# A mixture-of-experts schedule in which one more pair of experts works on gathered rows

## The reference, cut to what matters

```
scores = sigmoid(xt @ router_w)
biased = (scores + router_b).reshape(T, 4, 4)
best_group = argmax(top_k(biased, 2).sum(-1))         # one of four groups
local = top_k(biased of the best group, 2)            # two of its four experts
gate = scores of the two / their sum
y[token] += gate * ((silu(x @ w_gate[e]) * (x @ w_up[e])) @ w_down[e])
```

## Times and profile before

| | us |
|---|---|
| median of three runs | 1383.17 (1382.49 to 1383.35) |
| the profiled execution, its own time | 1383.31 |
| its span, first to last instruction | 1381.4 |
| TensorE busy in the span | 1321.1 (96%) |
| VectorE busy | 926.4 (67%) |
| ScalarE busy | 694.1 (50%) |
| expert pairs of layer 0, from the first matmul of pair 0's second tile to the first down of pair 7 | 194.2 |
| the same stretch of layer 1 | 195.4 |

### The profile page before, as it was taken

The page is one execution under the profiler, slowest core; times in us unless marked ns, Lnnn a source line. Parts: engine busy times, 40 slices in busy tenths (PEclk is TensorE's granted clock), DMA queues, the critical chain, the costliest instruction groups (busy, mean ns, idle before and its releaser), DMA issues.

```text
span 1381.4 us, 18142 instructions
## 1 busy us (share of the span) xinstructions
PE 1321.1 (96%) x7377; PEld 727.5 (53%) x7384; DVE 926.4 (67%) x1138; ACT 694.1 (50%) x710; POOL 99.3 (7%) x56
## 2 busy tenths in 40 slices
PE   6999999989999999999999999999989989999996
PEld 4686555446644445555667555444445545454442
DVE  5686776877764676465567575676866767766666
ACT  5466565335543454344457343555634664455552
POOL 0000000000000031000033003000004000300000
PEclk9999999999999999999999999999999999999999
DMA  9475434646665736475610445777927305576882
GB/s 308 138 249 159 146 122 158 223 160 205 211 207 194 254 134 224 162 252 191 207 62 2 153 153 183 242 252 234 351 100 266 110 0 186 180 229 231 271 270 96
DMA packets 152652, 258.07 MB, mean 187 GB/s; under 512 B 8881, under 2 KB 81532, under 8 KB 152572
## 3 DMA queue, kind: packets, MB, share of 16 engines
q1 hardware_dynamic: 152572, 256.96, 55.4%
HBM read 255.87 MB, written 1.07 MB: 186 GB/s over the span
## 4 chain that ended last, share of the span: by engine, by line
PE 84%; DVE 8%; DMA 2%; ACT 2%; issue 2%; DVEq 1%; POOL 1%; SPq 0%; POOLq 0%; ACTq 0%
PE ps L1192 15%; PE ps L1008 12%; PE ps L726 11%; PE ps L707 8%; PE ps L1273 6%; PE ps L1010 6%; PE ps L1031 6%; DVE w_ring L1883 3%; PE ps L744 3%; PE ps L968 2%; PE ps L1250 2%; PE ps L1128 1%; PE ps L671 1%; PE ps L1303 1%; ACT w_hi L1454 1%
## 5 line engine op out<-in xcount | busy, mean ns | idle before, releaser
L1883 DVE SCALAR_TENSOR_TENSOR w_ring<-w_ring,w_hi 128x2048 f16<-128x2048 f32 (+2 forms) x206 | 460.8, 2251 | 161.3 <-ACT w_hi L1454 160.1
L1454 ACT ACTIVATE w_hi<-w_ring 128x2048 f16<-128x2048 f32 (+2 forms) x206 | 381.5, 1864 | 220.7 <-PE ps L1031 50.9
L1008 PE MATMUL ps<-actT,w_hi 128*128 128x512 f16 x640 | 208.2, 379 | 1.1 <-issue 1.1
L1010 PE MATMUL ps<-actT,w_ring 128*128 128x256 f16 x640 | 174.4, 273 | 0.0
L1454 ACT ACTIVATE arena<-ps 128x512 f16<-128x512 f32 (+8 forms) x95 | 64.5, 694 | 168.0 <-PE ps L1010 76.6
L1192 PE MATMUL ps<-w_ring,arena 128*128 128x512 f16 x384 | 145.5, 379 | 0.0
L726 PE MATMUL ps<-w_hi,actT 128*128 128x512 f16 x448 | 137.1, 382 | 2.9 <-DVE w_ring L1883 2.9
L1192 PE MATMUL ps<-w_hi,arena 128*128 128x512 f16 x448 | 139.1, 379 | 0.0
L707 PE MATMUL ps<-w_hi,actT 128*128 128x512 f16 (+2 forms) x384 | 113.8, 373 | 2.9 <-DVE actT L1888 2.9
L1008 PEld LDWEIGHTS ps<-actT,w_hi 128*128 128x128 f16 x640 | 62.6, 98 | 77.1 <-issue 1.6
L1192 PE MATMUL ps<-arena 128*128 128x512 f16 x320 | 99.1, 379 | 0.0
(11 more groups left out here) (430 smaller groups left out, 1897.1 us busy)
## 6 DMA issues: line engine op xcount, KB each, us to landing
w_ring<-in_dil_w_in SPq DMA_DIRECT2D x36, 1024.0 KB, 5.2
w_ring<-in_w_ff SPq DMA_DIRECT2D x32, 1024.0 KB, 5.1
w_ring<-in_exp_w_gate SPq DMA_DIRECT2D x64, 512.0 KB, 4.2
w_ring<-in_exp_w_up SPq DMA_DIRECT2D x64, 512.0 KB, 5.2
w_ring<-in_exp_w_down SPq DMA_DIRECT2D x32, 1024.0 KB, 5.5
w_ring<-in_w_in SPq DMA_DIRECT2D x24, 1024.0 KB, 5.1
w_ring<-in_sb_w_in SPq DMA_DIRECT2D x12, 1024.0 KB, 5.7
w_ring<-in_w_branch SPq DMA_DIRECT2D x8, 1024.0 KB, 5.0
```

Source lines behind the costliest of these rows:

```text
L1008: pe.matmul(ps[:, bank + c, :], w_h[:, k, cols], aT[:, kk, :], start=(kk == 0), stop=False, skip_group_check=True)
L1010: ins = pe.matmul(ps[:, bank + c, 0:S], w_l[:, k, cols], aT[:, kk, 0:S], start=False, stop=(kk == KD - 1), skip_group_check=True)
L1454: return act.activation(dst, src, ACT.Copy, scale=scale)
L1883: dve.scalar_tensor_tensor(out=lo16(h)[:, 0:kn * c], in0=w_ring[:, h % RING, 0:kn * c], scalar=W_POW, in1=hi16(h)[:, 0:kn * c], op0=ALU.mu ...
```

## The change

The pairs become `0TXYAYZZ`. Pair 0 is still the first half of group 0 on all tokens. T is a half of the group that most tokens chose, and A is one more pair on all tokens: the other half of the top group, or of group 1 where the top group is group 0. X is the second half of group 0 (of group 1 in that case), on gathered rows, and Y and Z are the pairs of the other two groups, on gathered rows. So three pairs are full and five are few, and the gathered rows lie in three blocks of 128 (X, Y, Z) where there were two.

- The top group must be known before pair 1's gate and up weights can be loaded. `counts` moves ahead in pair 0 and waits for `r_best`; `top_group`, seven dependent instructions on VectorE ahead of `weigh(0, 0)`, writes the five group numbers; SP waits for them after the load of the second down of pair 0. The long ranking in `route` goes.
- In pair 0 the splits 6 and 7, which are the halves of pair 1's first `gate_up`, move behind `h_high(1, 0)` and `h_low(1, 0)`.
- `turn_slots` and two copies on ScalarE become `slot_rows` on TensorE and `slot_tokens`, four comparisons of 256 columns, on VectorE.
- Six gathers of 16 records with 128 columns replace four gathers of 8 records with 256 columns. The last two come behind pair 2's first `gate_up_few` and behind pair 1's second `down`. `gathered(5)` stands in pair 2 on both ScalarE and VectorE, ahead of the splits 4 and 5.
- In VectorE's `pair` the splits move as in ScalarE's, which is shown.

```diff
-GROUP_RANK = (0, 0, 2, 1, 2, 1, 3, 3)
-GROUP_PAIR = (0, 1, 0, 0, 1, 1, 0, 1)
-FIRST_FEW = 2
+PAIR_GROUP = "0TXYAYZZ"
+PAIR_HALF = (0, 1, 1, 0, 0, 1, 0, 1)
+SLOT_GROUPS = "XYZ"
+GROUP_NAMES = "TAXYZ"
+GROUP_TABLE = ((0, 4, 8, 12), (4, 4, 8, 12), (4, 0, 0, 0), (8, 8, 4, 4), (12, 12, 12, 8))
+GATHERS = 1
+GATHER_BANKS = (5, 4, 7, 6, 7, 6)
+ROUTE_PE = {"counts": 1, "tokens": 2, "rows": (3, 4, 5, 7, 8, 9), "gates": 6}
+ROUTE_DVE = {"best": 1, "groups": 2, "slots": 3, "tokens": 4, "rows": 5}
 
 
 def few(j):
 
-    return GROUP_RANK[j] >= 2
+    return PAIR_GROUP[j] in SLOT_GROUPS
...
-                    if GROUP_RANK[j] and len(group) == 1:
-                        sp.wait_ge(sig("route_dve"), 6 * layer + ROUTE_DVE["groups"])
-                        for r in range(3):
-                            group.append(sp.value_load(group_at[0:1, r:r + 1], min_val=4, max_val=12))
+                    if j == 2:
+                        for name in "XYAZ":
+                            group_load(name)
                     if few(j):
                         gate_up(j, 0)
                         down(j - 1, 1)
                     else:
                         if j:
                             down(j - 1, 1)
+                        if j == 1:
+                            sp.wait_ge(sig("route_dve"), 10 * layer + ROUTE_DVE["groups"])
+                            group_load("T")
                         gate_up(j, 0)
...
-                    c = GROUP_RANK[j] - 2
+                    c = block_of(j)
+                    if b == 0:
+                        gathered(2 * c + 1)
                     for i in range(2):
-                        if j == FIRST_FEW and b == 0:
-                            pe.wait_ge(sig("route_dve"), 6 * layer + ROUTE_DVE["rows"] + 2 * i + 1)
...
                     if b == 0 and slot_pairs(j):
-                        pe.wait_ge(sig("moe_y_lo"), 3 * layer + slot_pairs(j))
+                        pe.wait_ge(sig("moe_y_lo"), 4 * layer + slot_pairs(j))
+                    elif b == 0:
+                        pe.wait_ge(sig("route_dve"), 10 * layer + ROUTE_DVE["rows"] + 5)
...
                 def counts():
 
+                    pe.wait_ge(sig("route_dve"), 10 * layer + ROUTE_DVE["best"])
...
+                def slot_rows():
+
+                    pe.wait_ge(sig("route_dve"), 10 * layer + ROUTE_DVE["slots"])
+                    for t in range(T):
+                        ins = pe.matmul(ps[:, 5, t * P:(t + 1) * P], r_slot[:, t:t + 1].broadcast_to([P, P]), ident,
+                                        start=True, stop=True)
+                    ins.then_inc(sig("route_pe"), 1)
...
+                def gather(q):
+
+                    c = slice(q // 2 * P, (q // 2 + 1) * P)
+                    for i in range(4):
+                        k = 4 * (q % 2) + i
                         for t in range(T):
+                            ins = pe.matmul(ps[:, GATHER_BANKS[q], i * P:(i + 1) * P], x_tok[:, t, k * P:(k + 1) * P],
+                                            slot_of[:, t, c], start=(t == 0), stop=(t == T - 1))
...
                 def gather_gates():
-                    pe.wait_ge(sig("route_dve"), 6 * layer + ROUTE_DVE["rows"])
-                    for c in range(2):
+                    for c in range(3):
...
                         gate_up(j, 0, 1, True)
+                        counts()
                         gate_up(j, 1, 1, True, (0,))
                         turn(0, j)
-                        counts()
                         gate_up(j, 1, 1, True, (1,))
+                        pe.wait_ge(sig("route_dve"), 10 * layer + ROUTE_DVE["groups"])
+                        empty(3)
                     else:
-                        if j == 1:
-                            pe.wait_ge(sig("route_dve"), 6 * layer + ROUTE_DVE["slots"])
                         gate_up(j, 0, 1, True)
                         if by_slots(j - 1):
                             to_tokens(j - 1)
                         gate_up(j, 1, 0)
                         turn(0, j)
                         if gathers:
-                            turn_slots()
+                            slot_rows()
                         gate_up(j, 1, 1, True)
                     if j == NE // 2 - 1:
                         down(0, j, (0,))
...
                         down(1, j, (1,))
                         return
                     if gathers:
-                        pe.wait_ge(sig("route_act"), 5 * layer + ROUTE_ACT["tokens"])
+                        pe.wait_ge(sig("route_dve"), 10 * layer + ROUTE_DVE["tokens"])
                         pe.wait_ge(sig("x_full"), 2 * layer + 2)
                         gather(0)
                     put = down_few if by_slots(j) else down
...
                     if gathers:
                         gather(1)
                         gather(2)
+                        gathered(0)
+                        gather_gates()
                         pe.wait_ge(sig("moe_hT"), NE * layer + 2 + j * 2)
                         gather(3)
-                        gather_gates()
                     if few(j + 1):
                         gate_up_few(j + 1, 0)
                     else:
                         gate_up(j + 1, 0, 0)
+                    if gathers:
+                        gathered(2)
+                        gather(4)
                     put(1, j)
+                    if gathers:
+                        gathered(3)
+                        gather(5)
...
-                    gathers = j == FIRST_FEW - 1
+                    gathers = j == GATHERS
                     if j and by_slots(j - 1) and not few(j):
                         y_high(j - 1)
                     silu(0, j)
+                    if j == GATHERS + 1:
+                        gathered(5)
                     if j and by_slots(j - 1) and few(j):
                         y_high(j - 1)
                     split(4, j)
                     split(5, j)
                     h_high(0, j)
-                    if gathers:
-                        act.wait_ge(sig("route_pe"), 7 * layer + ROUTE_PE["tokens"])
-                        copy(tok16, ps[:, 5, :].rearrange("p (c s) -> p c s", c=2), SUM_POW / A_POW)
-                        copy(tok_of, ps[:, 5, S:2 * S]).then_inc(sig("route_act"), 1)
-                    next_split(6, j)
-                    if gathers or few(j):
+                    if j:
+                        next_split(6, j)
+                    if j == 0 or gathers or few(j):
                         silu(1, j)
                         if gathers:
                             gathered(0)
-                        next_split(7, j)
+                        if j:
+                            next_split(7, j)
                     else:
                         next_split(7, j)
                         silu(1, j)
                     if few(j):
                         next_split(8, j)
                     h_high(1, j)
+                    if j == 0:
+                        next_split(6, j)
+                        next_split(7, j)
                     if gathers:
                         for q in range(1, 4):
                             gathered(q)
                     if not few(j):
                         next_split(8, j)
+                    if gathers:
+                        gathered(4)
                     next_split(9, j)
...
+                def top_group():
+
+                    dve.wait_ge(sig("route_pe"), 9 * layer + ROUTE_PE["counts"])
+                    dve.tensor_copy(r_cnt, ps[:, 3, 0:12])
+                    dve.drain()
+                    dve.scalar_tensor_tensor(out=r_n, in0=rank0[:, 0, :], scalar=0.125, in1=r_cnt[:, 8:12],
+                                             op0=ALU.mult, op1=ALU.add)
+                    dve.drain()
+                    dve.tensor_reduce(r_max, g4(r_n), AX.X, ALU.max)
+                    dve.drain()
+                    dve.tensor_tensor(r_top, r_n, r_max.broadcast_to([P, 4]), ALU.is_ge)
+                    dve.drain()
+                    dve.tensor_tensor(g4(r_prod), group_table, r_top.unsqueeze(1).broadcast_to([P, 13, 4]), ALU.mult)
+                    dve.drain()
+                    dve.tensor_reduce(r_tab, g4(r_prod), AX.X, ALU.add)
+                    dve.drain()
+                    dve.tensor_copy(group_at[:, :], r_tab[:, 0:5]).then_inc(sig("route_dve"), 1)
...
+                def slot_tokens():
+                    dve.wait_ge(sig("route_pe"), 9 * layer + ROUTE_PE["tokens"])
+                    for c in range(3):
+                        dve.tensor_scalar(tok16[:, c, :], ps[:, 5, 0:S], slot_at[:, c:c + 1], SUM_POW / A_POW,
+                                          ALU.is_equal, ALU.mult)
+                    dve.tensor_scalar(tok_of, ps[:, 5, 0:S], slot_at[:, 2:3], None, ALU.is_equal)\
+                        .then_inc(sig("route_dve"), 1)
...
                     h_low(0, j)
+                    if gathers:
+                        slot_tokens()
...
```

(31 more changed lines are left out.)

129 lines of the change are left out of this document (62 added, 67 removed).

## The result

| | us |
|---|---|
| before, median of seven runs | 1381.91 (1380.39 to 1383.35) |
| after, median of seven runs | 1386.58 (1385.62 to 1388.61) |
| ratio | 1.0036, 95% interval 1.0025 to 1.0048 |
| profiled execution after, its own time and its span | 1388.02, 1386.2 |

The change makes the kernel slower by 0.36% by the ratio; the medians are 4.7 us apart. The forecast was 1382.8, no measurable change. So the time was missed by 3.8 us and the change by 5.2: -0.5 was forecast, +4.7 came. The profiled span grew by 4.8 us (1381.4 to 1386.2).

A forecast was written before the change was run, and what follows sets the result against it. TensorE's queue was taken to bound the expert stretches. Work -20.7, waits +15.6, landings +1.2 and clock +3.4 sum to -0.5 us, from 1383.31 to 1382.8 us; the range for 8 in 10 was 1379.3 to 1386.8.

The forecast's parts named there:

- The work: TensorE in both expert layers: fewer matmuls and shorter turns, less larger gathers and gates, -10.4 us per layer, -20.7 in all.
- top_group: Pair 0: seven VectorE instructions delay weigh(0, 0) to about 812.2; TensorE waits 1.8 us, with 0.15 at the turn before.
- the prediction's 0.17: Amount by which a wait's real delay exceeds its profile bracket, from one wait of 0.97 us that really was 1.13.
- The moved splits: Pair 0: splits 6 and 7 behind h_high and h_low delay pair 1's first gate_up by 4.9 us per layer.
- GpSimd's x_tok starts earlier and is not late: Pair 0: claim that GpSimd's x_tok starts earlier and is not late; no time was put down for it.
- The clock: Behind pair 0's 5 us wait the clock halves for 3.4 us, losing 1.7 us per layer, 3.4 in all.
- shorter waits lose the clock too: Rival, chance 0.13: waits of 2.1 us (pair 2) and 1.8 (pair 0) lose 1.7 each; two of four give 1386.2 us.
- Few behind few: Few pair after a few pair by slots, 2-3, 5-6 and 6-7: delays of 0.9, 1.0 and 0.3 us per layer.
- Landings: Few pairs: weight halves land late by a few tenths and push ScalarE; 1.2 us taken, bounds 0 and 3.
- the 7.0 of before: Old kernel's TensorE delays over both layers, 2.33 + 3.29 + 1.4 us, subtracted from the new waits of 22.6.
- The rival that the clock holds: Rival, chance 0.22: clock stays full through both layers' long waits, 1378.2 us, or 1379.4 with late landings.
- The DMA rival: Rival, chance 0.07: the five few pairs starve TensorE at 332 GB/s, 3 + 5.5 us instead of 1.2, 1390.1 us.

The follow-up runs named there:

- experiment 3: Changed kernel, but GpSimd starts x_tok only when VectorE has finished splits 6 and 7 of pair 0: 1382.00 us, ratio 1.0007 to before.
- experiment 1: Changed kernel with splits 6 and 7 of pair 0 put back ahead of h_high(1, 0) and h_low(1, 0): 1369.71 us, ratio 0.992 to before.
- experiment 2: Changed kernel with gathered(5) behind splits 4 and 5 of pair 2 on ScalarE and VectorE: 1381.46 us, ratio 0.9998 to before.
- experiment 4: Changed kernel with matmuls of zeros on TensorE, 24 in pair 0's wait and 8 in pair 2's: 1383.26 us, ratio 1.0011 to before.
- experiment 5: Changed kernel with the edits of experiment 3 and experiment 4 together: 1376.68 us, ratio 0.9966 to before.
- experiment 6: Changed kernel with the edit of experiment 1 and 8 matmuls of zeros in pair 2's wait: 1367.38 us, ratio 0.990 to before.
- experiment 7: Changed kernel with the edits of experiment 1 and experiment 2 together: 1364.69 us, ratio 0.9876 to before.
- experiment 8: Kernel of experiment 7 with VectorE's weigh(0, 3) ahead of the low part of pair 2's late half: 1363.76 us, ratio 0.9866 to before.

## Why the prediction was wrong

The forecast put -20.7 of work, +15.6 of waits, +1.2 of landings and +3.4 of clock against each other. By the traces:

- **The work: right.** A gather of 16 records took 1.79 us, so six take 10.7 (10.4 in the forecast's sum), and the 12 gate records 1.26. The work that went is 20.0 us: 13.83 and 0.44 less, 3.8 and 0.45 more in each layer.
- **top_group: right.** weigh(0, 0) started at 812.74 (812.2 forecast), the wait at down(0, 0) was 1.54 by its bracket, 1.7 with the prediction's 0.17 (1.8 forecast); the one at the turn was 0.5, not 0.15.
- **The moved splits: the place and the releaser right, the size wrong.** This is the first step that failed: "GpSimd's x_tok starts earlier and is not late". True, and GpSimd was not what anybody waited for; but its first instruction ran ahead of the first of the two splits on which TensorE now waited, and the splits took 7.88 and 8.22 us where the forecast had 4.49. The forecast's sum for turn(1, 0) to down(1, 0) is 0.49 + 4.9 + 5.2 + 1.7 for the clock = 12.3 us. With GpSimd out of the way it was 12.72 and 12.19 (experiment 3), with it 13.60 and 13.94. That is 1.3 and 1.6 more, 2.9 over both layers.
- **The clock: the second step that failed.** The sum has one loss in each layer, that of the 5 us wait, and leaves out the wait of 2.1 us in pair 2. It came as forecast (1.95 to 1.96 by its bracket), and the clock was 0.50 behind it in both layers: 1.68 more for `down_few`, 3.4 us over both. This is the rival "shorter waits lose the clock too" with two of its four, for which the prediction gave 1386.2; measured 1386.58. That the figures meet, and that the range to 1386.8 holds the result, is luck in part: the rival has nothing of GpSimd's 2.9 us, which the lower time before (1.4) and the 1.2 put down for landings nearly made up. The rival had 0.13, since the waits of before, 1.13 the longest that was looked at, kept the clock. The row at 508.75 with its 2.01 us was the one nearest in length, and it said the contrary. Two more of that length stand in the old trace outside the expert stretches, and the prediction did not read them; the granted clock was 0.50 and 0.51 in the 3.4 us behind them:

```profile
1016.74 0.58 PE L726 MATMUL ps<-w_hi,arena 128*128 128x512 f16 x1 [2.28 <-issue]
1112.20 1.51 PE L1421 MATMUL ps<-arena 128*64 128x256 f32 x8 [2.23 <-ACT arena L1847]
```

- **Few behind few: right or a little high.** With the 0.17, 0.8 us in pair 3 (0.8 forecast) and 0.4 each at pairs 6 and 7, where the prediction had 0.9 for the first turn of pair 6.
- **Landings: 1.2 forecast, at most 0.8 found.** The 0.4 at pair 6's first turn goes back to one in each layer: weigh (975.06) stands behind a split of VectorE, that one behind ScalarE's split of the same half, and this one waited 0.76 us for the half to land (0.80 in layer 1). Longer waits for landings come when other waits go or the clock holds (experiments 1, 2 and 4 to 7).

```profile
970.90 1.91 ACT L1493 ACTIVATE w_hi<-w_ring 128x2048 f16<-128x2048 f32 x1 [0.76 <-DMA w_ring<-in_exp_w_up]
972.85 2.29 DVE L1928 SCALAR_TENSOR_TENSOR w_ring<-w_ring,w_hi 128x2048 f16<-128x2048 f32 x1 [0.32 <-ACT w_hi L1493]
975.59 0.44 PE L1251 MATMUL ps<-mats,arena 128*128 128x128 f32 x2 [0.24 <-DVE arena L2723]
```


Together: -20.0 of work, +18.4 of waits (25.4 in the two layers, brackets and 0.17 each, landings and the two short waits inside `gate_up` among them, less the 7.0 of before), +6.3 of clock (1.5 and 1.7 in each layer) = +4.7 us, against 5.5 in the two stretches and 4.8 in the span. Experiment 4 corrects how this is shared: in pair 0 clock and slowed splits overlap, and the 1.5 of clock there is no cost of its own.

The rival that the clock holds was wrong at every one of the four waits. The DMA rival was wrong too: it had 8.5 us for late halves, and no more than 0.8 in these stretches goes back to a landing.

What stays open is when a short wait costs the clock. At `down_few(0, 2)` waits of 1.95 to 1.96 us cost it in five of six cases (two in the changed kernel, two in experiment 3, one of two in experiment 1). The length does not tell the sixth from the others, and no run was made to find out.

## What to carry to other kernels

Before a wait is made longer or an instruction is moved onto the path, look at what every other engine does at that moment, GpSimd above all: an engine that is never late can still slow the one that is waited for. Price a new wait of about 2 us as its length, and then, with a chance of its own, 1.7 us for the slow clock behind it (lost in 27 of 57 such waits here). Read every wait of that length in the old trace, and not only the first. A move that looks harmless in program order, two splits behind one small copy, cost 16.9 us of the 20 that the whole change saved; when a large saving shows as nothing, undo the moves one by one.

## What the runs showed of the hardware

**VectorE and GpSimd took turns.** The records of a split (2.24 us alone) and of one of GpSimd's tensor_tensor (2.33) overlap, but their lengths are those of two instructions one behind the other. In the changed kernel GpSimd was first (825.95), and split 6 ended 2.33 + 2.24 later, to 0.1 us, in both layers. In experiment 3 VectorE was first (829.00), and its two splits with GpSimd's first two instructions ended at 837.84, 8.84 us later, where their times alone add up to 4.48 + 4.66 = 9.14. By these sums it isn't a slower rate for both; the one that comes second stands still until the other's instruction ends. Who goes next is not shown: in the changed kernel and in experiment 3 they alternated one by one, but in the old kernel both splits went ahead of GpSimd's first instruction, though it had started at 828.86 and the second split only at 830.84. The Trainium skill (SBUF — State Buffer, "Who interferes with whom") states a rule for this: a VectorE instruction with two inputs in SBUF contends with a GpSimd instruction that reads SBUF, the port pair that they share is an exclusive lock, and whoever issues first has it for the whole instruction (the page writes the last of VectorE's two-port modes). These traces agree on the lock, with the numbers above; on the order the second split of the old kernel does not. The rule would have named the contention in advance, and the prediction did not weigh it.

**The clock.** Waits of 4.8 to 6.4 us lost it all six times (the changed kernel, experiments 2 and 3). Count as lost a stretch at 0.50 that began within the wait or up to 2.1 us behind it, and leave out the wait at the very start. Over the whole of all ten traces, the 68 waits of 1.0 to 1.6 us never did; of ten between 1.67 and 1.80 two did (behind layer 0's expert stretch, in experiments 7 and 8), of 57 between 1.95 and 2.38 it was 27, and of 21 between 2.6 and 3.03 it was 13. So between these lengths it went both ways, and even at one place: the wait of 2.28 us ahead of the block behind layer 0's experts lost the clock in four of the ten traces (before, changed, experiments 1 and 2) and kept it in six, with the same instructions there. Matmuls of zeros in the wait kept it at 1.00 in all ten places where they were put. The Trainium skill (TensorE: Matmul & The Clock Gate, "What's actually happening") says that activity releases the throttle; the zeros agree with it. They are no sure gain: in pair 0 alone they moved nothing (13.63 against 13.60 us).
